# The mixer's loop over 17 token tiles, written out in full instead of partly looped

## The chip, the cores and the metric

The kernel runs on one core of one Trainium2 chip. The metric is the device time of one execution in microseconds, the median over several runs. The five engines of the core each read their own stream of instructions: TensorE (PE in the profile; its weight loads are PEld), VectorE (DVE), ScalarE (ACT), GpSimd (POOL) and SyncE (SP, which here issues DMAs and nothing else). They meet only through semaphores. In the profile an engine's name with a q (PEldq, DVEq, SPq) stands for its sequencer, the part that reads the instructions and does branches, register arithmetic and DMA issues.

## The reference

One layer of a streaming encoder, for 2048 prompt tokens and 32 tokens of a running stream, width 1024, all in float32:

```
proj = x @ w_in                                  # 1024 -> 672 (attention part) + 1792 (RWKV part)
q    = rms_norm(c_q) @ w_uq ; ckv = rms_norm(c_kv) ; rotary on q_pe, k_pe
u    = pr + mu_shift * (prev_token(pr) - pr)     # r, k, v and three low-rank inputs
decay, a, g  from small matrices w2, a2, g2
s_t  = s_(t-1) * w_t + (s_(t-1) a_t) b_t' + v_t k_t' ;  y_t = s_t r_t     # 8 heads, state 64 x 64
rw   = (group_norm(y) + bonus) * g
m    = [attention(q, ckv) ; rw] @ w_o ;  h = layer_norm(alpha * x + m)
y    = layer_norm(alpha * h + experts(h))        # 4 groups of 8 experts, top 2 of one group
```

The first six lines, but for the attention itself, are what this document calls the mixer. Two outputs of it are the cached latents and the final states.

## The kernel before

The program runs six stages one after the other: `mixer`, `attention`, `router`, `dispatch`, `experts`, `combine`. Only the mixer is touched. Its 2048 + 32 tokens are NT = 17 tiles of 128 tokens (`SEQ // P + 1`), the last one padded. A tile passes through three bodies:

- `project` (letter a): the product with `w_in` (L806 on PE, 128x128 matmuls, by far the most of PE's work), the RMS norms (`rms_sums`, L847 to L852), the queries (L872, L880), the rotary part.
- `rwkv` (letter b): the low-rank products (L960, L961, L967), the Gram matrices (L984, L901), the inverse in five levels (L1009, L1018), then in turn G, SA, state and y (L916 to L951). The state goes from tile to tile, so that tile i+1's needs tile i's.
- `heads_out` (letter c): the group norm of y (two products on L894 with a DVE and an ACT step between), gate, store.

`layered` (L282) weaves them: in its step i, body a works on tile i, b on tile i-1 and c on tile i-2. Each engine has a string of letters (PE_ORDER, ACT_ORDER, VEC_ORDER, SP_ORDER) that says from which body its next piece comes; the order on an engine is that string and nothing else, the same in each step. Steps 0 and 1 are written out with constants. Steps 2 to 16, 15 of them, are one loop on each engine (`eng.Fori(deepest, count)`, L308). Steps 17 and 18, for the tiles still in b and c, are written out again. So there are 19 steps. The last instructions of a step on PE are the y products (L951), the first of the next are L806 matmuls of body a, for the next tile.

Waits count semaphore increments, so that the number waited for depends on the tile. In a written out step it is a constant; in the loop `Turn._wait` (L208) makes it out of the loop's register, with an instruction of register arithmetic. SP also works out the addresses of its DMAs from the register (`sp.snap`, L201 and the lines of the DMAs). SP loads masks, a flag and the initial state of a tile at L602 to L604 (`b_in`), once DVE is done with those of the tile before. On DVE, the step `u_pad` (L1128) waits for them, and what stands behind it on DVE is kk, u_r, u_v, the reciprocal of the group norm (L1248) and the sum of squares (L1067 to L1070) that PE waits for at L851.

Three later stages have loops too: the attention one of 4 turns (L240), the router one of 16 (`woven`, L268), the experts one of 31 turns on PE (L2310).

Of the kernel before, what the change touches and what calls it, by code (L numbers as in the profile page):

```python
# [281 lines left out]
def layered(eng, count, stages, order):  # L282

    for _, _, steps, _ in stages:
        if steps is not None:
            eng.sem_inc(steps.sem, steps.per)
    deepest = max(lag for _, lag, _, _ in stages)

    def once(i):
        gens, turns = {}, []  # L290
        for letter, lag, steps, body in stages:
            if isinstance(i, int) and not 0 <= i - lag < count:
                continue
            turns.append(Turn(eng, steps, i - lag))
            gens[letter] = body(turns[-1])
        for c in order:
            if c in gens:
                next(gens[c], None)
        for g in gens.values():
            for _ in g:  # L300
                pass
        for t in turns:
            if t.own is not None:
                t.own.whole()

    for i in range(deepest):
        once(i)
    with eng.Fori(deepest, count) as i:  # L308
        once(i)
    for i in range(count, count + deepest):  # L310
        once(i)


# [70 lines left out]
def mixer(nc, io, scr):  # L384
    ahead = scr["first_of_attention"] = first_of_attention(nc)

    with ExitStack() as ctx:
# [128 lines left out]
        def _(sp):  # L516
# [107 lines left out]
            def heads_out(t):  # L624
# [4 lines left out]
                rwkv_out.go(sp.dma_start(scr["rwT"].rearrange("(c p) n -> p c n", p=P)[:, :, col], ys[:]))  # L629

            layered(sp, NT, (("a", 0, None, project), ("b", 1, None, rwkv), ("c", 2, None, heads_out)), SP_ORDER)
            for d in (mla_out, rwkv_out, edge_out, state_out):
                sp.wait_ge(d.sem, d.done(NT - 1))
# [3 lines left out]
        def _(g):  # L637
# [14 lines left out]
            def rwkv(t):  # L652
# [13 lines left out]
                yield  # L666

            layered(g, NT, (("b", 1, pol, rwkv),), "")

        @block.scalar  # L670
        def _(a):
# [113 lines left out]
            def heads_out(t):  # L785
# [9 lines left out]
                t.mark(ins, "y_gain")  # L795

            layered(a, NT, (("a", 0, aact, project), ("b", 1, act, rwkv), ("c", 2, oact, heads_out)), ACT_ORDER)

        @block.tensor
# [1830 lines left out]
```

How the kernel before makes its waits and increments, by code:

```python
    def _wait(self, counts, name, turn):  # L204
        v = self.known.get((counts.sem.name, name, turn))
        if v is None:
            v = counts.done(self.i + turn, name) if name else counts.done(self.i + turn)
        self.eng.wait_ge(counts.sem, v)
# [1 line left out]
    def do(self, ins, name):  # L210
        self.own.mark(ins, name)
        self.eng.wait_ge(self.own.sem, self.own.done(self.i, name))
# [301 lines left out]
        @block.sync  # L515
# [11 lines left out]
                consts.go(sp.dma_start(w_wa[hs], io["w_wa"][hs, 512 * r:512 * r + 512]))  # L527
                consts.go(sp.dma_start(cst[hs], io["cst"].rearrange("p (a n) -> p a n", a=7)[hs, :, hs]))
                consts.go(sp.dma_start(one64[hs], io["ident"][hs, hs]))
                consts.go(sp.dma_start(levs[hs], io["levs"].rearrange("p (a n) -> p a n", a=LEVELS)
                                      [hs, 0:LEVELS - 1, 32 * r:32 * r + 32]))
            consts.go(sp.dma_start(w_g[:], io["w_g"]))
            for k in (1, 0, 2):
                c0, c1 = w_cols[k]
                sp.dma_start(w_in[:, :, c0:c1], w_src[:, :, c0:c1]).then_inc(w_part[k], 16)
            sp.dma_start(w_uq[:], io["w_uq"].rearrange("p (a n) -> p a n", a=CQ)).then_inc(w_queries, 16)
            sp.wait_ge(first_x, 2)
            def x_load(tile):
# [91 lines left out]
            for d in (mla_out, rwkv_out, edge_out, state_out):  # L632
                sp.wait_ge(d.sem, d.done(NT - 1))
            sp.wait_ge(x_in.sem, x_in.done(NT + 1))
# [813 lines left out]
        @block.scalar  # L1448
        def _(a):
            a.wait_ge(setup, 6)
            def turn(t):
```

## Time and profile before

| what | value |
|---|---|
| median of 3 runs | 3352.1 us (3346.84 to 3356.85) |
| the profiled execution | 3348.55 us, of it the span from first to last instruction 3346.5 us |
| PE busy over the span | 2949.8 us, 88% |
| mixer (PE's matmuls from 5.4 us to about 1447 us) | 43% of the span |
| steps 2 to 16 of the mixer on PE | 144.6 us to 1366.45 us |
| mean granted TensorE clock over the span | 0.947 |

The page's second part shows the span in 40 slices of 84 us; slices 1 to 17 are the mixer. PE is at nine tenths in all of them but the first and the last, DVE at six, ACT at three. A digit is a mean over 84 us, though, and one step of the loop is about as long, so a stop that comes once in each step cannot be seen there; a window of one step, or a list of waits, shows it. Step i of the loop ends on PE with the last L951 matmul: 222.18 us for step 2, 304.03 us for step 3, and so on to 1366.45 us for step 16.

### The profile page before, as it was taken

The page shows a single profiled execution, that of the slowest core. Times are in us where ns is not written, and L with a number is a line of the kernel's source. Part 1 is how long each engine was busy: PE and PEld are TensorE (multiplying, and loading weights), DVE is VectorE, ACT ScalarE, POOL GpSimd, SP SyncE. Part 2 cuts the span into 40 slices and gives each one's busy share as a digit, 9 for nine tenths or more (in the row PEclk, how much of TensorE's full clock was granted, in tenths as well). Part 3 has the DMA queues.
Part 4 walks back from the last instruction along what each step waited for, and adds up shares of the span by engine and source line. Part 5 has one row for each costly group of instructions (what it writes and reads, how often), then busy time and mean ns, then how long its engine had stood idle before and what let it go on. Part 6 is the DMA issues. An engine that isn't in the chain of part 4 may idle for free. (4 is left out here: it accounts for less than half of the span.)

```text
span 3346.5 us, 74487 instructions
## 1 busy us (share of the span) xinstructions
PE 2949.8 (88%) x26600; PEld 2235.1 (67%) x26601; DVE 1750.7 (52%) x3820; ACT 971.1 (29%) x2500; POOL 581.9 (17%) x875
## 2 busy tenths in 40 slices
PE   7999999999999999669898898989975999999991
PEld 6888888888888888545555555545544776666770
DVE  1666666666666666648686886822234222222225
ACT  2333333333333333224343434412210111111115
POOL 0000000000000000000000000001113555545650
PEclk9999999999999999779999999999987999999995
DMA  6111111111211111420101000033325898886447
GB/s 188 34 37 36 36 36 36 36 37 37 38 37 37 36 36 36 96 84 1 38 1 35 5 21 15 1 108 128 125 85 219 272 342 289 246 257 171 100 93 244
DMA packets 337220, 310.25 MB, mean 93 GB/s; under 512 B 235200, under 2 KB 290528, under 8 KB 322528
## 3 DMA queue, kind: packets, MB, share of 16 engines
q1 hardware_dynamic: 315424, 238.88, 23.4%
q0 software_dynamic: 21504, 67.13, 8.9%
q8 instruction: 226, 3.70, 0.5%
q14 instruction: 66, 0.54, 0.1%
HBM read 208.12 MB, written 84.42 MB: 87 GB/s over the span
## 5 line engine op out<-in xcount | busy, mean ns | idle before, releaser
L806 PE MATMUL mx_bank<-mx_xT,mx_w_in 128*128 128x128 f32 x5168 | 661.2, 286 | 71.1 <-issue 52.4
L806 PEld LDWEIGHTS mx_bank<-mx_xT,mx_w_in 128*128 128x128 f32 x5168 | 618.8, 198 | 144.1 <-issue 121.0
L1497 PE MATMUL at_bank<-pl_kT,pl_qT 128*128 128x512 f32 (+5 forms) x656 | 293.8, 534 | 2.4 <-DVE at_vals L1621 2.4
L1469 ACT ACTIVATE at_PQ<-at_bank,at_nms 128x512 f32<-128x512 f32 (+5 forms) x328 | 192.8, 596 | 277.6 <-DVE at_nms L1597 199.9
L2288 PE MATMUL ex_down<-ex_wd,ex_hT 128*128 x512 | 235.6, 603 | 28.1 <-ACT ex_hT L2217 26.4
L2165 POOL DMA_INDIRECT ex_x<-scr_hx,ex_idx x256 | 247.0, 965 | 68.3 <-issue 59.4
L2264 PE MATMUL ex_gate<-ex_wg,ex_xT 128*128 x1024 | 233.2, 381 | 19.0 <-SPq L2137 18.8
L2264 PEld LDWEIGHTS ex_gate<-ex_wg,ex_xT 128*128 128x128 f32 x1024 | 195.4, 191 | 72.9 <-issue 49.0
L2224 ACT ACTIVATE ex_y<-ex_down,ex_gcol 128x512 f32<-128x512 f32 x128 | 81.0, 683 | 543.8 <-POOL ex_gcol L2172 227.2
L2264 PE MATMUL ex_up<-ex_wu,ex_xT 128*128 x1024 | 231.6, 379 | 0.0
L1640 DVE COPY at_PT<-at_bank 128x512 f32<-128x512 f32 (+3 forms) x328 | 196.8, 601 | 55.0 <-PE at_bank L1509 41.0
L1528 PEld LDWEIGHTS at_bank<-at_PT,at_vals 128*64 128x64 f32 (+1 forms) x2208 | 118.4, 138 | 155.2 <-issue 80.9
L2333 DVE STREAM_TRANSPOSE ex_xT<-ex_x 128x256 f32<-128x256 f32 x256 | 141.1, 609 | 147.2 <-DMA ex_x<-scr_hx,ex_idx 147.2
L1509 PE MATMUL at_bank<-pl_at_ident,at_PQ 128*128 128x128 f32 x1104 | 187.4, 285 | 32.4 <-ACT at_PQ L1469 15.9
L1509 PEld LDWEIGHTS at_bank<-pl_at_ident,at_PQ 128*128 128x128 f32 x1104 | 126.8, 142 | 120.3 <-issue 57.2
L2264 PEld LDWEIGHTS ex_up<-ex_wu,ex_xT 128*128 128x128 f32 x1024 | 190.3, 191 | 23.2
L657 POOL TENSOR_TENSOR mx_AR<-mx_u,mx_ep 128x512 f32<-128x512 f32 x17 | 20.0, 1176 | 1036.2 <-DVE mx_kh L1154 1036.2
L1593 DVE TENSOR_REDUCE at_mx<-at_bank 128x1 f32<-128x512 f32 (+5 forms) x328 | 188.4, 574 | 11.8 <-PE at_bank L1497 7.3
L1528 PE MATMUL at_bank<-at_PT,at_vals 128*64 128x128 f32 (+1 forms) x2208 | 168.0, 285 | 26.0 <-DVE at_o_sb L1615 25.8
L2288 PEld LDWEIGHTS ex_down<-ex_wd,ex_hT 128*128 128x128 f32 x512 | 96.6, 192 | 132.9 <-issue 130.8
L702 ACT ACTIVATE mx_pr<-mx_bank 128x256 f32<-128x256 f32 (+1 forms) x68 | 37.0, 544 | 510.1 <-PE mx_bank L806 500.8
L2340 DVE SCALAR_TENSOR_TENSOR ex_th<-ex_th,ex_gate 128x256 f32<-128x256 f32 x64 | 26.8, 419 | 261.3 <-ACT ex_th L2212 201.0
(316 smaller groups left out, 4738.6 us busy)
## 6 DMA issues: line engine op xcount, KB each, us to landing
ex_wg<-in_w_eg SPq DMA_DIRECT2D x32, 1024.0 KB
ex_wu<-in_w_eu SPq DMA_DIRECT2D x32, 1024.0 KB
ex_wd<-in_w_ed SPq DMA_DIRECT2D x32, 1024.0 KB
mx_x<-in_x SPq DMA_DIRECT2D x76, 128.0 KB, 4.0
pl_ro_x<-in_x SPq DMA_DIRECT2D x17, 512.0 KB, 3.9
scr_hx<-ro_h SPq DMA_DIRECT2D x17, 512.0 KB, 2.7
scr_acc<-ro_ha SPq DMA_DIRECT2D x17, 512.0 KB, 2.9
co_r<-scr_acc SPq DMA_DIRECT2D x17, 512.0 KB, 5.6
```

The lines of the kernel that those rows point to most:

```text
L806: ins = pe.matmul(dst, w_in[:, k, col:col + n], xT[:, k, :], start=(k == 0), stop=(k == KC - 1))
L1469: ins = a.activation(PQ[:, n % NP, 0:full], b[:, 0:full], ACT.Exp, bias=bias, scale=SCALE, accum_out=sums[:, j, h, 1 + gi:2 + gi])
L1497: t.mark(pe.matmul(bank[n % SB][:, 0:wd], qT[h][keys(h), j * P:(j + 1) * P], kT[h][keys(h), k0 * P:k0 * P + wd], start=True, stop=True), f ...
L1509: ins = pe.transpose(bank[SB + n % TB][0:rows, c:c + P], PQ[:, n % NP, c:c + rows], ident[:, :])
L1528: ins = pe.matmul(bank[7][64 * h:64 * h + 64, 0:P], vals[0:rows, k0 + s, 64 * h:64 * h + 64], PT[0:rows, m % NPT, s, :], start=(gi == 0 an ...
L1593: t.do(v.tensor_reduce(mx[:, 1 + gi:2 + gi], b[:, 0:wd], AX.X, ALU.max), f"max{n}")
L1640: ins = v.tensor_copy(PT[:, n % NPT, 0:full, :], b[:, 0:full * P].rearrange("p (a n) -> p a n", a=full))
L2165: x_in[s].go(g.indirect_dma_start(x[s][:, k, :], None, rows, bass.IndirectOffsetOnAxis(ap=idx[s][:, k:k + 1], axis=0)))
L2224: ins = a.activation(y[s][:, 512 * n:512 * n + 512], down_b[n][:, :], ACT.Copy, scale=gcol[s][:, 0:1])
L2264: ins = pe.matmul(b[s][:, 0:FE], xT[s][:, k, :], wv[:, k * FE:(k + 1) * FE], start=(k == 0), stop=(k == KC - 1))
L2288: ins = pe.matmul(down_b[n][:, :], hT[s][:, m, :], wv[:, m * D + n * 512:m * D + (n + 1) * 512], start=(m == 0), stop=(m == FC - 1))
L2333: ins = v.transpose(xT[s][:, :, 32 * h:32 * h + 32], x[s][:, h, :].rearrange("p (i k) -> p k i", k=KC))
```

## The change

`layered` no longer makes a loop. All 19 steps are written out, on all five engines, with constants for every wait and address. The order of the work on each engine, the buffers, the DMAs and their sizes stay as they are. All other stages keep their loops and their text.

```diff
-    for i in range(deepest):
-        once(i)
-    with eng.Fori(deepest, count) as i:
-        once(i)
-    for i in range(count, count + deepest):
+    for i in range(count + deepest):
         once(i)
```

The lines of the changed file stand four earlier than those of before (L806 is L802 there).

On PE, from the end of step 1 into step 2. L951 is body b's last product, L806 the first of body a, L894 the group norm; an ISA row at L208 or L308 is register arithmetic:

```order
L951 MATMUL mx_bank<-mx_AR,mx_Sp 64x64 x2
L951 MATMUL mx_bank<-mx_BB,mx_SA 64x64 x2
L951 MATMUL mx_bank<-mx_MK,mx_vt 64x64 x2
L308 UNCONDITIONAL_BRANCH
L308 ISA
L208 ISA
L806 MATMUL mx_bank<-mx_xT,mx_w_in 128x128 x8
L208 ISA
L894 MATMUL mx_bank<-mx_ys,mx_cst 64x512 x2
```

```order
L947 MATMUL mx_bank<-mx_AR,mx_Sp 64x64 x2
L947 MATMUL mx_bank<-mx_BB,mx_SA 64x64 x2
L947 MATMUL mx_bank<-mx_MK,mx_vt 64x64 x2
L802 MATMUL mx_bank<-mx_xT,mx_w_in 128x128 x8
L890 MATMUL mx_bank<-mx_ys,mx_cst 64x512 x2
L802 MATMUL mx_bank<-mx_xT,mx_w_in 128x128 x8
```

The branch and the register instructions are gone, the matmuls stand in the same order. The end of the loop's body on PE was one REGISTER_ALU and one COMPARE_AND_BRANCH at L308; where they stood, the next step's L802 matmuls follow now as above.

On SP, at the same place: the last load of x and the store of the state (L622) of one step, then the loads for u_pad (L602 to L604) and for body a of the next:

```order
L542 DMA mx_x<-in_x 32x32x32 x4
L622 DMA out_state_out<-mx_S 128x256
L308 UNCONDITIONAL_BRANCH
L308 ISA
L201 ISA
L602 ISA
L602 DMA mx_masks<-in_masks 128x256
L603 ISA
L603 DMA mx_keep_s<-in_keep 128x1
L604 DMA mx_s_init<-in_s_init 128x256
L201 ISA x3
```

```order
L538 DMA mx_x<-in_x 32x32x32 x4
L618 DMA out_state_out<-mx_S 128x256
L598 DMA mx_masks<-in_masks 128x256
L599 DMA mx_keep_s<-in_keep 128x1
L600 DMA mx_s_init<-in_s_init 128x256
L562 DMA mx_first<-in_first 128x15
```

The DMAs keep their order; the register instructions between them are gone.

## Rows read from the trace of the kernel before

**Rows 1.** The page: busy us by engine, and PE's tenths in 40 slices.

```profile
PE 2949.8 (88%) x26600; PEld 2235.1 (67%) x26601; DVE 1750.7 (52%) x3820; ACT 971.1 (29%) x2500; POOL 581.9 (17%) x875
...
PE   7999999999999999669898898989975999999991
```

**Rows 2.** PE's waits in steps 3 to 16: in total, times, longest us.

```profile
PE mx_bank L806 <- issue: 52.4, 14, 3.9
PE mx_bank L937 <- ACT mx_SA L776: 8.0, 14, 0.6
PE mx_bank L847 <- ACT mx_kp L693: 5.2, 14, 0.5
PE mx_bank L851 <- DVE mx_sq L1070: 4.4, 7, 1.2
```

**Rows 3.** Timeline of PE at the first back edge: start, us, instructions, [idle before].

```profile
225.86 3.78 PE L806 MATMUL mx_bank<-mx_xT,mx_w_in 128*128 128x128 f32 x16 [3.67 <-issue]
```

**Rows 4.** Loop's own instructions on L308: duration ns min/median/max.

```profile
L308 PEldq COMPARE_BRANCH  x15: 83/4174/4297, 221.5 to 1365.7; - x15
...
L308 DVEq COMPARE_BRANCH  x15: 50/56/67, 222.8 to 1367.0; - x15
```

**Rows 5.** Windows behind that back edge: us, busy by engine, PEclk, DMA.

```profile
225.80:229.60 3.80, 3.74 (x18) 3.53 (x18) 0.00 (x0) 1.24 (x3) 0.00 (x0) 0.50 0.84 132
229.60:233.70 4.10, 4.10 (x21) 2.37 (x20) 1.86 (x6) 1.40 (x4) 0.00 (x0) 0.70 0.42 104
233.70:240.00 6.30, 6.30 (x67) 5.04 (x67) 5.80 (x12) 6.24 (x15) 0.00 (x0) 1.00 0.08 21
```

**Rows 6.** Windows: step 2, step 3, step 10, steps 3 to 16.

```profile
144.60:222.20 77.60, 74.51 (x1087) 66.90 (x1086) 50.46 (x91) 25.77 (x60) 5.26 (x4) 1.00 0.20 38
222.18:304.03 81.85, 77.41 (x1087) 68.94 (x1086) 50.56 (x92) 25.77 (x60) 5.25 (x4) 0.96 0.19 37
794.50:875.64 81.14, 76.12 (x1086) 68.41 (x1086) 50.44 (x92) 25.77 (x60) 5.25 (x4) 0.98 0.19 37
222.18:1366.45 1144.27, 1074.18 (x15205) 959.59 (x15204) 707.09 (x1275) 360.81 (x840) 73.50 (x56) 0.97 0.19 37
```

**Rows 7.** Timeline of PE, its first matmuls of step 2.

```profile
144.53 2.05 PE L806 MATMUL mx_bank<-mx_xT,mx_w_in 128*128 128x128 f32 x16
```

**Rows 8.** PE's waits in step 2, all of them.

```profile
PE mx_bank L847 <- ACT mx_kp L693: 1.5, 1, 1.5
PE mx_bank L851 <- DVE mx_sq L1070: 1.0, 1, 1.0
PE mx_bank L937 <- ACT mx_SA L776: 0.6, 1, 0.6
```

**Rows 9.** Timelines of SP and DVE in step 2.

```profile
144.38 4.14 SPq L542 DMA_DIRECT2D mx_x<-in_x  x4
148.56 0.67 SPq L622 DMA_DIRECT2D out_state_out<-mx_S  x1
149.95 0.40 SPq L602 DMA_DIRECT2D mx_masks<-in_masks  x1
...
153.14 0.17 DVE L1128 TENSOR_TENSOR mx_u<-mx_u,mx_masks 128x4 f32<-128x4 f32 x1 [3.54 <-DMA mx_s_init<-in_s_init]
```

**Rows 10.** The issue of L622 in steps 3 to 16.

```profile
L622 SPq DMA_DIRECT2D out_state_out<-mx_S x14: 1472/1984/2768, 227.5 to 1290.5; - x14
```

**Rows 11.** PE's branches of the other loops: duration ns min/median/max.

```profile
L240 PEldq COMPARE_BRANCH  x4: 82/3532/3842, 1640.8 to 2190.5; - x4
...
L268 PEldq COMPARE_BRANCH  x16: 83/215/238, 2228.6 to 2474.5; - x16
...
L2310 PEldq COMPARE_BRANCH  x31: 76/211/248, 2591.6 to 3262.0; - x31
```

**Rows 12.** Window of one turn of the experts' loop.

```profile
2612.80:2634.10 21.30, 21.30 (x87) 15.81 (x86) 5.93 (x12) 3.85 (x8) 12.69 (x20) 1.00 0.81 246
```

**Rows 13.** The page's DMA queues: packets, MB, share.

```profile
q8 instruction: 226, 3.70, 0.5%
```

## The prediction, as it was made before the changed kernel ran

> **What bounds the kernel now.** I read the page first: PE is busy 88% of the span and DVE, the next, 52%; PE's row of slices stands at nine tenths all through the mixer [rows 1]. So in this stage time goes only where PE stops or slows down. The slices can't show that, so next came the waits of PE over steps 3 to 16. There are four, and one outweighs the rest: 52.4 us in 14 stops in front of L806, put down to "issue", that is to nothing another engine did [rows 2]. The timeline shows one: L806 starts at 225.86 us after 3.67 us of nothing, so that the step before ended at 222.19 us [rows 3]. The instructions of the loop itself explain it: PE's branch back takes 4.17 us in the median, while its shortest, the one that falls through at the end, takes 0.08 us. The same branch on DVE takes 0.06 us [rows 4]. Nothing but the branch lies between the two matmuls, and PE has nothing queued that could cover it.
>
> The windows behind the stop show a second cost. The granted clock is 0.50 (1.2 GHz) for the first 3.8 us, 0.70 on average in the next 4.1 us, and 1.00 (2.4 GHz) from then on [rows 5]. Before it fell, PE had stood still for the 3.67 us of the branch. The reader is to see that 16 matmuls of L806 take 3.78 us there [rows 3] and 2.05 us where PE did not stop before them [rows 7].
>
> **What a step without the branch takes.** The trace holds one. Step 2 runs the loop's body for the first time, and is entered from written out code, not by a branch back: step 1 ends on PE at 144.60 us, and L806 is at work from 144.53 us, with no idle time noted before it [rows 7]. Its window is 77.60 us, PE is busy 74.51 us in it and the clock is 1.00 throughout. The 14 steps behind it take 1144.27 us, 81.73 us each, with 76.73 us busy [rows 6]. The matmul counts are equal (1087 against 15205/14 = 1086), so it is the same work.
>
> **The sum, part by part, for each of 14 steps.**
>
> - The branch: 52.4/14 = 3.74 us go. No wait for another engine stands behind them in that place, since step 2 starts without one.
> - The slow clock: 76.73 - 74.51 = 2.22 us of PE's busy time go.
> - Given back: while PE stood still, ACT and DVE went on, and so they come late for L847 and L851 once PE doesn't stop. In the loop these waits cost (5.2 + 4.4)/14 = 0.69 us a step [rows 2]; in step 2 they cost 1.5 + 1.0 = 2.5 us [rows 8]. That is 1.8 us back.
> - The wait at L937 for SA stays at 0.6 us in both [rows 2, 8].
> - Net: 3.74 + 2.22 - 1.8 = 4.16 us; straight from the windows it is 81.73 - 77.60 = 4.13 us. Fourteen of them are 57.8 us.
>
> The register instructions on PE, ACT and DVE I cost at nothing: they lie beside matmuls and vector work that is under way, and step 2, which has them all, serves as the measure. Without them it can only be a little less. Steps 0, 1, 17 and 18 were written out already, and the loop's end falls through in 0.08 us. The entry into the loop costs PE nothing [rows 7]. So none of these adds a term.
>
> **The term that I can't read off** is whether steps 3 to 16 will look like step 2 in the 2.5 us. L851 waits for DVE, and DVE in step 2 sat idle 3.54 us until 153.14 us for the loads of masks and state. SP issued these late: four loads of x for 4.14 us, the store of the state for 0.67 us, then 0.72 us of loop set-up (148.56 + 0.67 to 149.95) [rows 9]. The set-up goes; if that alone counts, DVE is 0.7 us earlier and the wait at L851 falls to about 0.3 us, which makes 4.85 us a step, 67.9 us in all. Against it, the store's issue takes 1.98 us in the median in steps 3 to 16 [rows 10], 1.3 us longer than in step 2. If that is how SP runs from step 3 on, with set-up or without, DVE is up to 1.3 us later, and the step gains 2.8 us, 39.6 us in all. The two about cancel, so I take step 2 as it stands.
>
> On the supply of code, the Trainium skill ("Runtime: NRT & Kernel Launch", section "Instruction fetch mechanics") says that a taken branch out of the pages held must fetch its target first, and that the crossing from one 16 KiB block to the next in straight code is "mostly hidden". The trace agrees with the first by its 4.17 us [rows 4]. The word "mostly" speaks against the change, since the same blocks still have to come; if one crossing of each step cost what a branch costs, the gain would be nil. That is the first rival below.
>
> **The rivals.**
>
> 1. *The stall moves instead of going.* PE would then wait for its next piece of code somewhere in a written out step too, 3.7 us once a step, and the time stays at about 3349 us. For it: the page shows 226 instruction packets of 3.70 MB for 53201 PE and PEld instructions [rows 1, 13], about 235 to a packet if they are all PE's, so that a step of 2173 needs some nine, and none of them is hidden by being held. Against it: PE's waits in step 2 have no issue stop in the list at all [rows 8], though the same 2173 instructions streamed through. 3%.
> 2. *Nothing is given back.* ACT and DVE may keep up once their sequencers do no register work: then 3.74 + 2.22 = 5.96 us a step go, 83.4 us in all, 3265 us. For it: several steps of the loop show no wait at L851 at all (7 of 14) [rows 2]. Against it: there PE came 4 to 6 us later. 15%.
> 3. *The clock falls again.* If SP is late as in rows 10, the waits at L847 and L851 are 1.5 and 2.3 us with two short matmul groups between, close to the 3.7 us of the branch. In step 2, where they were 1.5 and 1.0 us, the clock stayed at 1.00 [rows 6, 8]. If it dropped, the step would lose 76.12 - 74.51 = 1.6 us (step 10) to 77.41 - 74.51 = 2.9 us (step 3) [rows 6], and of the 2.8 us of that case 1.2 to -0.1 us would be left: 3332 to 3350 us, about 3338 us. 8%.
> 4. *Later loops begin to miss* (slower). The mixer's code grows and everything behind it on PE stands at other addresses. The loops of the router and the experts now branch back in 0.21 us [rows 11]; if where a body lies among the fetched pieces decides that, some could come to cost what L308 and L240 cost (4.17 and 3.53 us). At 3.7 us each, 15 + 30 branches are 167 us, so that the time would be 3291 + 167 = 3458 us; from 57.8/3.7 = 16 branches on the kernel is slower than before, so the experts' loop alone is enough. Against it: one turn of the experts is 87 + 86 instructions on PE [rows 12], less than one packet's 235, so such a body lies in two pieces at the most, wherever it starts; the bodies that miss have 2173 and more. 4%.
>
> The page of the skill that I named gives a window of two 16 KiB blocks in one sentence and 128 KiB for PE in another. By either rival 4 would not happen; no row here tells the two apart.
>
> **How the numbers follow.** The profiled execution took 3348.55 us, its span 3346.5 us. Less 57.8 us it is 3290.8 us. The median of the runs is 3.55 us above the profiled execution, which would make 3294.3 us; I say 3292 us. The forecast's own range is 39.6 to 67.9 us of gain with 4 us of scatter to each side: 3277 to 3313 us, 70%. Rival 2 lies at 3255 to 3277 us (15%; 3255 if the 0.69 us of waits go as well), rival 3 at 3332 to 3350 us (8%), rival 1 at 3349 us (3%), rival 4 above (4%). A range of 3262 to 3316 us leaves out a part of rival 2 and the others and holds a little over 80%. A difference of about 0.3% (10 us) is what a measurement of this kernel can tell from none: faster by more than that, under 3342 us, is the forecast, rival 2 and most of rival 3, 92%; within it, rival 1 and the rest of 3, 4%; slower, 4%.
>
> **What would show it.** Right: no compare and branch of the mixer in PE's sequencer; no issue stop in front of the first L802 of a step; a clock of 1.00 in every window of one step; steps 3 to 16 of about 77.6 us, all alike; waits at L843 and L847 (L847 and L851 before) of about 2.5 us a step instead of 0.7 us; attention, router and experts as long as before. Wrong: steps of 76 us or less (the waits were not given back); a step's clock under 1.00; issue stops inside a step; a branch at the router's or the experts' loop of several us.

## The result, and the profile after

The changed kernel takes 3301.35 us in the median of 4 runs (3294.75 to 3307.45), against 3349.55 us (3346.84 to 3356.85) for the kernel before; that is the median of four runs, the three of the table above and one of 3346.99 us. The ratio is 0.9852, with a 95% interval of 0.9821 to 0.9884: 1.5% less time. It ran once more later, beside other kernels: 3298.81 us, ratio 0.9849 (0.9830 to 0.9868). The forecast was 3292 us.

The profiled execution took 3294.75 us, its span is 3292.9 us, 53.6 us shorter than before. On the page, PE's busy time fell with the count of its instructions unchanged, and so did the packets of the queue that carries instructions (columns as in [rows 1, 13]):

```profile
PE 2928.2 (89%) x26600; PEld 2219.5 (67%) x26601; DVE 1745.8 (53%) x3820; ACT 973.1 (30%) x2500; POOL 589.0 (18%) x875
...
PE   7999999999999999589898988899957999989990
...
q8 instruction: 192, 3.15, 0.4%
```

PE is busy 21.6 us less [rows 1]. Of the 226 packets of queue q8 [rows 13], 34 are gone. The queue is PE's: the pages show 226 in each of the three kernels in which PE keeps this loop as it was, and 192 in each that has it written out on PE and PE's later loops as before, whatever the other engines do. The packets of q14, the other instruction queue, rose from 66 to 94.

PE's waits in steps 3 to 16, now from 221.32 us to 1309.24 us (in total, times, longest us), answer to [rows 2]:

```profile
PE mx_bank L843 <- ACT mx_kp L689: 20.6, 14, 1.5
PE mx_bank L847 <- DVE mx_sq L1066: 10.8, 10, 2.0
PE mx_bank L933 <- ACT mx_SA L772: 8.1, 14, 0.6
```

The 52.4 us of "issue" are gone. The two waits for ACT and DVE, which were L847 and L851 before, went from 9.6 us to 31.4 us. The timeline of PE where step 3 begins has L802 right behind the last product of step 2, where [rows 3] had 3.67 us of nothing:

```profile
221.01 0.31 PE L947 MATMUL mx_bank<-mx_MK,mx_vt 64*64 64x64 f32 x4
221.25 1.60 PE L802 MATMUL mx_bank<-mx_xT,mx_w_in 128*128 128x128 f32 x12
```

The windows of steps 3, 4, 5 and 16, and of steps 3 to 16 together (us, busy by engine, then PEclk, DMA share and GB/s), answer to [rows 6]:

```profile
221.32:299.93 78.61, 75.91 (x1088) 68.14 (x1087) 49.95 (x91) 25.80 (x60) 5.63 (x4) 0.98 0.20 38
299.93:376.40 76.47, 74.43 (x1088) 66.92 (x1087) 50.55 (x92) 25.80 (x60) 5.64 (x4) 1.00 0.20 39
376.40:456.41 80.01, 75.93 (x1087) 67.62 (x1087) 49.85 (x91) 25.80 (x60) 5.62 (x4) 0.98 0.19 37
1232.89:1309.24 76.35, 74.31 (x1086) 66.75 (x1086) 50.42 (x91) 25.79 (x60) 5.63 (x4) 1.00 0.20 39
221.32:1309.24 1087.92, 1048.49 (x15205) 942.09 (x15204) 702.85 (x1274) 361.15 (x840) 78.87 (x56) 0.99 0.20 38
```

A step takes 1087.92/14 = 77.71 us instead of 81.73 us. The steps are not alike: 76.35 to 80.01 us, and in some the clock fell again.

The longest, step 5, shows where the difference comes from. SP, DVE and PE in it, from their timelines (start, us, instructions, [idle before]), answer to [rows 9]:

```profile
376.90 3.22 SPq L538 DMA_DIRECT2D mx_x<-in_x  x4
380.16 0.68 SPq L618 DMA_DIRECT2D out_state_out<-mx_S  x1
380.88 0.44 SPq L598 DMA_DIRECT2D mx_masks<-in_masks  x1
...
386.35 0.17 DVE L1124 TENSOR_TENSOR mx_u<-mx_u,mx_masks 128x4 f32<-128x4 f32 x1 [5.05 <-DMA mx_s_init<-in_s_init]
389.76 3.35 DVE L1244 RECIPROCAL mx_yq<-mx_yq 128x512 f32<-128x512 f32 x1
394.28 0.28 DVE L1066 TENSOR_TENSOR mx_sq<-mx_sq 128x128 f32<-128x128 f32 x1
...
392.15 0.43 PE L843 MATMUL mx_bank<-mx_kp,mx_sel 128*64 128x128 f32 x2 [1.47 <-ACT mx_kp L689]
394.62 0.49 PE L847 MATMUL mx_bank<-mx_sq,mx_rmsw 128*128 128x128 f32 x2 [2.03 <-DVE mx_sq L1066]
```

SP is prompt, but the data lands late; DVE idles 5.05 us, and PE pays 2.03 us of that. In step 4 DVE idled 2.64 us there, and PE did not wait at L847. From its issue to its landing, the load of the initial state (L600) takes 2.1 to 4.4 us over steps 3 to 16:

```profile
DMA to landing us min/median/max: 2.1/2.8/4.4
```

### The profile page after: what moved, and what is told of

The parts are those of the page before. It is cut to its first block and busy times, and to the rows that moved or that the text cites. A ratio compares the mean times of both kernels' runs of the same rounds, so it can differ in the third digit from the quotient of the medians.

```text
span 3292.9 us, 71371 instructions
## 1 busy us (share of the span) xinstructions
PE 2928.2 (89%) x26600; PEld 2219.5 (67%) x26601; DVE 1745.8 (53%) x3820; ACT 973.1 (30%) x2500; POOL 589.0 (18%) x875
## 5 line engine op out<-in xcount | busy, mean ns | idle before, releaser
L802 PE MATMUL mx_bank<-mx_xT,mx_w_in 128*128 128x128 f32 x5168 | 645.4, 282 | 17.7 <-DVEq L286 14.2
L802 PEld LDWEIGHTS mx_bank<-mx_xT,mx_w_in 128*128 128x128 f32 x5168 | 603.7, 194 | 83.5 <-issue 60.4
L1505 PE MATMUL at_bank<-pl_at_ident,at_PQ 128*128 128x128 f32 x1104 | 189.0, 287 | 34.1 <-ACT at_PQ L1465 17.5
```

The source lines that it names most:

```text
L802: ins = pe.matmul(dst, w_in[:, k, col:col + n], xT[:, k, :], start=(k == 0), stop=(k == KC - 1))
L1505: ins = pe.transpose(bank[SB + n % TB][0:rows, c:c + P], PQ[:, n % NP, c:c + rows], ident[:, :])
```

## The experiments

The experiments ran on three chips, each beside the kernel before on the same chip: pe_only, all_but_pe, pe_by_three and router_by_four where that takes 3357.59 us, the others where it takes 3350.15 or 3349.28 us. Ratios are to that neighbour. The whole time differs by some 8 us between the chips, so a comparison between kernels goes by the ratio or by the length of a step.

**Which engine's loop?** In `layered`, a flag per engine decides whether steps 2 to 16 are a loop (body as before) or written out:

```diff
-def layered(eng, count, stages, order):
+def layered(eng, count, stages, order, looped=False):
...
-    for i in range(count + deepest):
-        once(i)
+    if looped: ...  # as before
+    else: ...       # all written out
```

pe_only:

> All 19 mixer steps are written out on PE alone; SP, POOL, ACT and DVE keep their loops, register waits and register addresses. Theory (PE's back edge is what cost): as the changed kernel, 3295 to 3310 us, steps 3 to 16 of about 77.7 us on PE and no branch of the mixer in PE's sequencer. SP keeps its set-up of 0.72 us before the loads for u_pad, which may add up to 0.7 us a step, 10 us in all. Rival (the gain came from constant waits and addresses on the other engines): about 3350 us, steps of 81.7 us.

It took 3341.56 us, ratio 0.9941 (0.9920 to 0.9963): 0.6% less time. Neither theory holds as written. Steps 3 to 16 take 1125.10/14 = 80.36 us. PE's waits in them:

```profile
PE mx_bank L855 <- DVE mx_sq L1074: 25.9, 14, 2.9
PE mx_bank L851 <- ACT mx_kp L697: 23.2, 14, 1.7
PE mx_bank L941 <- ACT mx_SA L780: 8.1, 14, 0.6
```

The stops for the branch are gone, all of them; but the two waits take 49.1 us, 17.7 us more than in the changed kernel, and PE's busy time in the window is 1067.85 us, 19.4 us more than there, at a mean clock of 0.97:

```profile
221.64:1346.74 1125.10, 1067.85 (x15204) 959.52 (x15204) 701.36 (x1275) 361.12 (x840) 73.53 (x56) 0.97 0.19 37
```

SP's timeline at the end of step 3 of this kernel (303.2 us) shows the difference to the changed kernel. Between the store's issue and the masks' there is 1.01 us (306.67 + 0.63 to 308.31), where the changed kernel has 0.04 us:

```profile
306.67 0.63 SPq L626 DMA_DIRECT2D out_state_out<-mx_S  x1
308.31 0.38 SPq L606 DMA_DIRECT2D mx_masks<-in_masks  x1
```

Over steps 3 to 16 the masks' load is issued 5.97 us after PE's end of the step before in the mean, against 4.55 us in the changed kernel, and DVE starts u_pad at 9.55 us against 8.63 us. Step 2 of this kernel, where SP comes from written out code, takes 77.48 us; the steps behind it take 80.36 us.

all_but_pe:

> The opposite: PE keeps its loop over steps 2 to 16, the other four engines are written out. Theory: no gain, 3343 to 3352 us, 14 branches back of about 4.2 us on PE, clock at 1.2 GHz behind each, steps of about 81.7 us. Rival (constant waits and addresses elsewhere are the gain): about 3301 us.

3357.25 us against 3357.59 us for the kernel before beside it, ratio 0.9995 (0.9985 to 1.0005): no change; steps 3 to 16 take 81.69 us. PE's branch and its stops are there as before:

```profile
L309 PEldq COMPARE_BRANCH  x15: 83/4037/4237, 220.0 to 1363.7; - x15
```

```profile
PE mx_bank L810 <- issue: 50.5, 14, 3.8
PE mx_bank L941 <- ACT mx_SA L780: 8.1, 14, 0.6
PE mx_bank L851 <- ACT mx_kp L697: 6.6, 14, 0.5
```

So the other four engines give nothing alone, PE gives 0.6% alone, and all five together 1.5%. The parts are not additive, because PE's branch hides what makes the others late.

pe_and_sp (ACT, DVE and POOL keep their loops):

> The mixer written out on PE and SP; ACT, DVE and POOL keep their loops. pe_only took 80.4 us a step and not 77.7: SP issued the masks' load 5.9 us after the step's end on PE instead of 4.6 us, DVE began u_pad at 9.5 us instead of 8.5 us, the wait before the RMS sums was 1.9 us instead of 0.8 us, and the clock fell in more of the steps. Theory (SP's set-up and address arithmetic is what pe_only lacked): the load at about 4.6 us, steps of 77.7 to 78.3 us, 1.3% less time than before. Rival (register arithmetic on ACT and DVE makes them late): steps stay at about 80 us, with the load early and u_pad's DVE work late all the same.

3303.31 us, ratio 0.9866 (0.9842 to 0.9890), the same as the changed kernel within the intervals. PE's waits in steps 3 to 16:

```profile
PE mx_bank L851 <- ACT mx_kp L697: 23.4, 14, 1.7
PE mx_bank L941 <- ACT mx_SA L780: 8.1, 14, 0.6
PE mx_bank L855 <- DVE mx_sq L1074: 4.3, 8, 1.3
```

The masks' load is issued at 4.48 us again, and the wait for DVE falls from 25.9 to 4.3 us. So it was for the most part SP's address arithmetic and loop set-up that pe_only lacked: 80.36 - 78.51 = 1.85 us a step. Between 78.51 us and the 77.71 and 78.07 us of the changed kernel's two traces, 0.4 to 0.8 us are left for the loops of ACT, DVE and POOL together. The theory was a little too good for the step, 78.51 us instead of 77.7 to 78.3 us: the wait for ACT stays at 1.67 us instead of 1.47 us, and the clock fell in more steps (1.2 GHz for 47.8 us of the 14 steps, in 13 of them, against 17.1 us in the changed kernel's first trace and 34.1 us in its second).

**How much does one branch back cost?** PE in 5 turns of 3 steps, all else written out:

```diff
-        with eng.Fori(deepest, count) as i:
-            once(i)
+        with eng.Fori(0, (count - deepest) // 3) as j:
+            for k in range(3):
+                once(j * 3 + (deepest + k))
```

> The other four engines written out, PE in a loop of 5 turns with 3 steps each: 4 branches back instead of 14 or none. Theory (a price per branch): the changed kernel plus 4 times 57.2/14 = 4.1 us, so 16 us more than it, about 3317 us; 4 stops of about 3.7 us on PE. Rival (the cost of a branch grows with the code that it jumps over, here three times as much): 4 stops of up to 11 us, 3330 us or more. Rival (PE's register arithmetic in each wait is what slows a loop): it is all still there, so 3340 us or more.

3319.07 us, ratio 0.9882 (0.9852 to 0.9912). The profile has 4 stops, 4.2 us each, behind branches of 4.53 us in the median:

```profile
L309 PEldq COMPARE_BRANCH  x5: 83/4526/4727, 376.2 to 1323.4; - x5
```

```profile
PE mx_bank L811 <- issue: 16.8, 4, 4.3
PE mx_bank L852 <- ACT mx_kp L698: 15.8, 14, 1.4
PE mx_bank L942 <- ACT mx_SA L781: 8.1, 14, 0.6
PE mx_bank L856 <- DVE mx_sq L1075: 6.9, 8, 1.7
```

The four steps with a stop take 81.2 to 82.6 us, as every step did before; the other ten 76.3 to 79.3 us. All of PE's register arithmetic is still in place, so that one isn't the price. A jump over three times as much code costs 4.5 us instead of 4.2 us. The price per branch is best read inside this trace: the four steps take 81.94 us in the mean and the ten others 77.51 us, 4.43 us each, where 4.1 us was expected. The 3319.07 us agree with the expected 3317 us less well than they seem to, since this chip is the slower one: the ratio is 0.3% above the changed kernel's 0.9852, some 10 us and not 18 us, and its interval allows both.

**What PE waits for in the branch.** The traces hold the packets of q8, which carry PE's instructions. In each of the 14 slow branches of the kernel before (4.04 to 4.30 us) two of them start; this is the queue in the first (window 221.5 to 225.7 us), and in the first slow one of pe_by_three (376.2 to 380.9 us):

```profile
q8 instruction: 2, 0.03, 3.7%
```

```profile
q8 instruction: 2, 0.03, 4.0%
```

In straight code, step 3 of the changed kernel, 8 packets come in 78.61 us, none closer than 5.8 us to the last, and PE has no issue stop at them. In the attention's three slow branches (3.44 to 3.84 us) one packet starts. In the branches of 0.2 us of the router and the experts none does. So the stop is the fetch of the code branched to.

**Do PE's remaining waits hide anything?** norms_later moves one piece of PE's work behind the first projection group, some 3.8 us of matmuls later:

```diff
-                t.w(aact, "kpe_part")
-                t.mark(pe.matmul(... kpe_sum ...), "kpe_sum")
-                ...                                    # rms_sums
-                yield
...
                     t.mark(ins, f"pr_proj{k}")
                     yield
+                    if k == 3:
+                        norms()                        # kpe_sum, rms_sums
+                        yield
```

> The changed kernel with one piece of PE's work moved: kpe_sum and rms_sums (L843 to L848) come after the two column blocks of the first projection group instead of before it, about 3.8 us of matmuls later. In the changed kernel they wait 1.47 us for ACT in each of steps 2 to 16 and 0 to 2.03 us for DVE. Theory (these waits are PE's own idle time and nothing hides behind them): both vanish, 15 times about 2.3 us, 35 us, and the clock no longer falls inside the mixer's steps, 5 to 10 us more: about 3258 us. Rival (what the RMS norm releases on ACT and DVE is as urgent, so a wait comes up later in the step): half of it or less, 3280 to 3301 us.

3249.85 us, ratio 0.9699 (0.9682 to 0.9715), 8 us less than the theory's 3258 us. Steps 3 to 16 take 74.79 us:

```profile
PE mx_bank L936 <- ACT mx_SA L772: 8.1, 14, 0.6
PE mx_bank L893 <- issue: 0.3, 1, 0.3
```

```profile
218.67:1265.78 1047.11, 1038.71 (x15204) 935.54 (x15204) 703.27 (x1274) 361.15 (x840) 78.92 (x56) 1.00 0.21 40
```

Both waits are gone, none but a single stop of 0.3 us has come, and the clock is 1.00 through all 14 steps. Steps 2 to 16 are 44.8 us shorter than in the changed kernel's first trace, and so are the two profiled executions (3294.75 and 3249.95 us), at the upper end of the theory's 40 to 45 us. The 51.5 us between the medians hold another 6.6 us by which the changed kernel's median lies above its profiled execution.

tile_in_early issues the three loads for u_pad of the next tile behind the store of the k tokens on SP:

```diff
+                if t.i + 1 < NT:
+                    t.w(vec, "state_in")
+                    tile_in(t.i + 1)                   # masks, keep_s, s_init
```

> The changed kernel with the loads for u_pad (masks, flag, initial state) of the next tile issued after the store of this tile's k tokens instead of behind the loads of x and the store of the state. Theory (DVE's idle time in front of u_pad makes the wait at L847): DVE's wait of 3 to 4 us goes, the wait at L847 of 0 to 2.0 us (mean about 0.8) goes, the wait at L843 for ACT of 1.47 us stays; 15 times 0.8 us and some clock, 10 to 20 us: about 3287 us. Rival (the wait at L847 comes from DVE's order of work and not from the loads): within 5 us of 3301 us.

3268.69 us, ratio 0.9754 (0.9738 to 0.9770); I had expected 3287 us. The wait at L847 is gone and the one for ACT is left, exactly as expected, 20.5 us in 14 steps:

```profile
PE mx_bank L849 <- ACT mx_kp L695: 20.5, 14, 1.5
PE mx_bank L939 <- ACT mx_SA L778: 8.1, 14, 0.6
```

The rest of the gain inside the mixer's steps is the clock. It stays at 1.00 with the 1.47 us stop alone, and all 14 steps take 76.3 to 76.5 us:

```profile
219.98:1289.00 1069.02, 1040.42 (x15205) 935.49 (x15204) 705.37 (x1274) 361.12 (x840) 78.91 (x56) 1.00 0.20 39
```

Steps 3 to 16 are 18.9 us shorter than in the changed kernel's first trace: 10.8 us of the wait and 8.1 us of PE's busy time. Steps 2 to 16 are 21.3 us shorter, so that some 11 us of the 32.7 us between the medians lie outside them and are not explained by the move. The scatter of the changed kernel's steps came from these loads; why single ones land up to 2 us later was not tested.

both_moves:

> Both of the moves (norms later on PE, loads for u_pad early on SP). Theory: if norms_later takes both waits away, the early loads add little, about 3255 us; if it leaves some for DVE, the two add up. PE's busy time at the full clock is 74.5 us a step and with the 0.6 us at SA the floor of a step is 75.1 us, against 77.7 us now: 14 or 15 times 2.6 us, 38 us, is the most.

3245.29 us, ratio 0.9689 (0.9667 to 0.9710), the fastest median, but within the interval of norms_later. Its step is 1046.63/14 = 74.76 us, as in norms_later, 0.3 us under the floor of 75.1 us that I had worked out: PE is busy 74.2 us in it and not 74.5 us, and waits 0.58 us at SA.

**The moves with loops left in place.**

> PE alone written out (as pe_only), and the RMS sums after the first projection group (as norms_later). Theory (after PE's branch only those two waits and the clock that they bring down are left, whatever makes ACT and DVE late): steps of about 74.8 us, as in norms_later, 3% less time than before, with four engines still in their loops. Rival (late engines hold PE up elsewhere as soon as this wait is gone): steps of 76 us or more and a wait at another line.

3252.19 us, ratio 0.9712 (0.9696 to 0.9728). Steps of 75.11 us: SP, ACT, DVE and POOL can keep their loops. The clock is 1.00 throughout. 3.8 us in all are left, at another line. The profile puts them to "issue", but in each of the six L901 starts 0.10 us after GpSimd has written the mx_t that it reads (L665), and no q8 packet is near, so it is a late neighbour after all: the rival had the right idea and far too large a price:

```profile
PE mx_bank L944 <- ACT mx_SA L780: 8.1, 14, 0.6
PE mx_bank L901 <- issue: 3.8, 6, 1.0
```

> The kernel before with its loops on all engines, and the RMS sums after the first projection group. Theory (in the loop the branch's 3.7 us cover ACT and DVE already): only the 0.69 us of waits a step go, 15 times that, 5 to 12 us, 0.2 to 0.4%; the 14 stops for the branch and the clock behind them stay. Rival (the waits are worth as much here as in the changed kernel): 1.5% or more.

3325.89 us, ratio 0.9932 (0.9913 to 0.9950), 0.7% less, between the two theories; the 14 branches of 4.0 to 4.2 us are there as before. The step takes 80.39 us, 1.34 us less. The waits explain 0.69 us of it; the other half is the clock, at 1.2 GHz for 54.6 us of the 14 steps instead of 75.1 us, a change that I had counted at nothing.

> The changed kernel once more, beside the others on one chip, so that they can be compared: 1.2 to 1.8% less time than before, steps 3 to 16 of 77.7 us give or take 0.5 us. If the length of its steps comes from waits of chance length for SP's loads, single steps differ by up to 4 us as in the first trace, and at other places.

Steps 3 to 16 took 1092.99/14 = 78.07 us, from 76.35 to 80.98 us, and the clock was low for 34.1 us. The ratio is given above.

**How much code may a loop have before its branch costs?** One run each; PE's loop in the router unrolled by 4 and by 8 in the changed kernel:

```diff
-    with eng.Fori(0, count - 1) as i:
+    with eng.Fori(0, (count - 1) // many) as j:
+        for n in range(many):
+            i = j * many + n
```

> The changed kernel with PE's loop in the router in 4 turns of 4 tiles instead of 16 of one: its body grows from 118 recorded instructions to some 470, more than one fetched piece of 235 to 256 and no more than two or three. It has 3 branches back. If only what lies within about two pieces is held, some of them may take 3.5 to 4.2 us instead of 0.21 us; if more is held (as one sentence of the skill's page has it, 2048 instructions), all take 0.21 us. The time changes by less than 15 us either way.

> As router_by_four, with 2 turns of 8 tiles: a body of about 940 recorded instructions, some four fetched pieces, and one branch back. If about two pieces are held it takes 3.5 to 4.2 us; if 2048 instructions are held it takes 0.21 us. The time changes by less than 10 us.

PE's branches at L268, by four and by eight:

```profile
L268 PEldq COMPARE_BRANCH  x4: 76/217/252, 2228.1 to 2424.8; - x4
```

```profile
L268 PEldq COMPARE_BRANCH  x2: 76/160/244, 2293.8 to 2424.9; - x2
```

The window of one turn of eight:

```profile
2294.00:2424.90 130.90, 130.90 (x449) 69.46 (x448) 36.66 (x80) 29.40 (x40) 18.76 (x8) 1.00 0.36 126
```

A body of 897 matmul and load instructions still branches back in 0.24 us. The mixer's, with 2173, doesn't. Nor is the body fetched a second time: from 2262.5 to 2437 us, which holds the branch and the whole second turn, the only queue with packets is

```profile
q1 hardware_dynamic: 14487, 21.25, 34.3%
```

So all of it was still held; the packets of its first turn start at 2192.9, 2225.7 and 2262.4 us (the page has 195 in all, against 192). The single times are 3308.28 us, ratio 0.9853 to its neighbour's 3357.59 us, and 3297.97 us, ratio 0.9844 to 3350.15 us: as the changed kernel's, for what one run can tell.

## Why the prediction was right, and where it was not

- *The branch.* Forecast 3.74 us a step. Gone to the last stop, brought back four times by pe_by_three, and left whole by all_but_pe. Shown, and the packets of q8 show what it waits for. The prediction's some 235 instructions to a packet were too many, since the router's and the experts' turns are not fetched again; no term hangs on it.
- *The clock.* Forecast 2.22 us a step and 1.00 in every window. Measured: PE busy 1048.49/14 = 74.89 us against 76.73 us, 1.84 us. The forecast of 1.00 everywhere was wrong: in 5 of the 14 steps, and in step 2, the clock fell once for 3.4 us. Rival 3 had described such falls, and its lower price was right (75.9 - 74.3 = 1.6 us), but not how often. Its condition doesn't decide it either: the clock fell in three steps whose second wait was 1.9 to 2.0 us, not in a fourth with 1.91 us, and in two with 0.65 and 0.45 us.
- *What is given back.* Forecast 2.5 us of waits a step, measured 31.4/14 = 2.24 us. Net: a step of 77.71 us against 77.60 us; the mixer from step 3 to 16 went from 1144.27 us to 1087.92 us, 56.35 us against the 57.8 us of the sum.
- *The open term.* The store's issue, feared at 1.98 us, went down to 0.64 to 1.41 us (in the second trace to 1.93 us at most). I had put its length to how SP runs; it goes with PE's loop: 0.58 to 0.87 us in pe_only, where SP has its loop, and 1.73 to 2.65 us in all_but_pe, where SP is written out. And the landing of the loads has a scatter of its own, so the step is neither step 2's everywhere nor one of the two ends.
- *The register instructions, costed at nothing.* This was meant for PE, ACT and DVE. On PE it holds: in pe_by_three all of it is there, and PE is busy 74.36 us in a step at the full clock, against 74.31 us. The loops of ACT and DVE, with POOL's, cost 0.4 to 0.8 us a step (pe_and_sp), so a little was missed. The error is with SP. I argued that step 2 serves as the measure, and gave SP's loop 0.72 us at most. Step 2 was entered from written out code with SP on time. With SP in its loop and PE out of it, the masks' load comes 1.4 us later and the step is 80.36 us (pe_only); with SP written out too it is 78.51 us. SP's loop is worth nothing as long as PE stops for its branch (all_but_pe, 0.9995) and 1.85 us a step once it doesn't. The sum came out right because the change removed both.
- *3292 us against 3301 us.* The mixer gave what it should. The profiled execution took 3294.75 us where the sum had 3290.8 us: 1.4 us more in steps 3 to 16, and 3.7 us more in what follows them (1983.7 us instead of 1980.0 us), less 1 us before them. The other 5.4 us are the median: I put it 1.2 us above the profiled execution, and it lies 6.6 us above. What follows step 16 took 1977 to 1984 us in ten of the fourteen profiles and 1985 to 1996 us in the four from one chip, so it goes with the chip more than with the kernel.
- *The rivals.* 1 (the stall moves): refuted, no issue stop in a step, though 8 packets of code come in it. 2 (nothing given back): not this kernel, but norms_later shows that the room was there, and it is 41 us wide. 4 (later loops miss): refuted; the branches at L268 and L2306 take 0.21 us as before, and the router's still does with eight times the body.

## What to carry to other kernels

Look for the loop's branch in the sequencer's own rows: a stop called "issue" once a turn on the busiest engine, with a branch of several us under it, is code that has to be fetched again (packets of the engine's instruction queue start in the branch), and the clock that falls behind it can cost half as much again. Write out only that engine, but expect that the stop has been covering late neighbours; put independent work in front of the waits that come up, which was worth more here (1.5% in the changed kernel, 2.3% with PE alone written out) than writing out all the other engines (0.9%). An edit that alone changes nothing may be a condition for another one, so test an engine's share both ways.

## What the runs showed that I had not expected

The clock reacts to small differences. With one stop of 1.47 us a step it never fell (tile_in_early). With the same stop and 0 to 2.0 us shortly behind it, it fell in 5 steps of 14 in one trace and in 7 in another. With 1.67 us and a mean of 0.3 us (pe_and_sp) it fell in 13. What sets this apart was not settled. And PE's branch back costs 0.24 us for a body of 897 instructions and 4.2 us for one of 2173; where between the two the change lies was not tried.
